# Expert loop of a mixture-of-experts stage: one bias table, other POOL slots, transposes of the next rows at other places

## The reference

```python
gu = xb @ w_gu[e] + b_gu[e]                       # (128,1024) @ (1024,2048)
g = jnp.minimum(gu[:, ::2], SWIGLU_LIMIT)
u = jnp.clip(gu[:, 1::2], -SWIGLU_LIMIT, SWIGLU_LIMIT)
h = (u + 1.0) * (g * jax.nn.sigmoid(SWIGLU_ALPHA * g))
return h @ w_dn[e] + b_dn[e]                      # (128,1024) @ (1024,1024)
```

## Time and profile before

| what | us |
|---|---|
| median of 3 runs | 3178.49 (3175.48 to 3181.2) |
| the profiled execution's own time | 3171.74 |
| its span, first to last instruction | 3169.9 |
| PE busy in the span | 2691.3 (85%) |
| DVE busy | 1818.4 (57%) |
| ACT busy | 1352.0 (43%) |
| POOL busy | 963.4 (30%) |
| the 32 items, about | 1694 to 3077 |

### The profile page before, as it was taken

The page is one execution under the profiler, slowest core; times in us unless marked ns, Lnnn a source line. Parts: engine busy times, 40 slices in busy tenths (PEclk is TensorE's granted clock), DMA queues, the critical chain, the costliest instruction groups (busy, mean ns, idle before and its releaser), DMA issues. The chain is left out here.

```text
span 3169.9 us, 37221 instructions
## 1 busy us (share of the span) xinstructions
PE 2691.3 (85%) x13181; PEld 1995.3 (63%) x13181; DVE 1818.4 (57%) x2326; ACT 1352.0 (43%) x1417; POOL 963.4 (30%) x435
## 2 busy tenths in 40 slices
PE   7698999799969999797836999999999999999970
PEld 4465555689945555586334777777777777776750
DVE  0433444317755555210245877777877777777766
ACT  1232322214334444100004666666666666666650
POOL 0001121000012222000023555555555555555553
PEclk9899999799989999898957999999999999999995
DMA  2103343222232112332027888889889889889854
GB/s 79 56 1 120 132 166 117 56 69 81 67 98 83 31 57 57 93 80 98 25 74 270 315 319 320 314 310 322 310 320 321 311 311 321 307 324 320 307 202 162
DMA packets 240551, 580.65 MB, mean 183 GB/s; under 512 B 25660, under 2 KB 114812, under 8 KB 235336
## 3 DMA queue, kind: packets, MB, share of 16 engines
q1 hardware_dynamic: 221984, 503.18, 46.5%
q0 software_dynamic: 17168, 76.05, 6.5%
q10 hardware_dynamic: 1296, 0.01, 0.0%
HBM read 546.88 MB, written 32.18 MB: 183 GB/s over the span
## 5 line engine op out<-in xcount | busy, mean ns | idle before, releaser
L2048 ACT ACTIVATE w_hi<-w_raw 128x2048 fp32r<-128x2048 f32 x290 | 556.5, 1919 | 241.0 <-PE banks L1994 241.0
L2089 DVE TENSOR_TENSOR w_lo<-w_raw,w_hi 128x2048 fp32r<-128x2048 f32 x226 | 570.2, 2551 | 120.0 <-ACT w_hi L2048 120.0
L1994 PE MATMUL banks<-w_hi,x_hi 128*128 128x512 f32 x1024 | 349.4, 424 | 96.4 <-POOL b_two L1953 89.7
L1958 POOL TENSOR_TENSOR w_lo<-w_raw,w_hi 128x2048 fp32r<-128x2048 f32 x64 | 302.1, 4721 | 344.9 <-ACT w_hi L2048 344.9
L1994 PE MATMUL banks<-w_hi,x_lo 128*128 128x512 f32 x1024 | 337.2, 412 | 0.0
L1994 PE MATMUL banks<-w_lo,x_hi 128*128 128x512 f32 x1024 | 334.9, 410 | 0.0
L1994 PEld LDWEIGHTS banks<-w_hi,x_hi 128*128 128x128 f32 x1024 | 206.1, 207 | 162.9 <-issue 121.7
L2089 DVE TENSOR_TENSOR w_lo<-mergedT,w_hi 128x2048 fp32r<-128x2048 f32 x98 | 233.5, 2410 | 104.5 <-ACT w_hi L2048 104.5
L2048 ACT ACTIVATE w_hi<-mergedT 128x2048 fp32r<-128x2048 f32 x98 | 187.8, 1917 | 182.5 <-PE banks L1994 117.9
L1994 PEld LDWEIGHTS banks<-w_lo,x_hi 128*128 128x128 f32 x1024 | 206.0, 201 | 46.8
L1994 PEld LDWEIGHTS banks<-w_hi,x_lo 128*128 128x128 f32 x1024 | 204.5, 200 | 45.6
(11 more groups left out here) (399 smaller groups left out, 5087.0 us busy)
## 6 DMA issues: line engine op xcount, KB each, us to landing
w_raw<-in_exp_w_gu SPq DMA_DIRECT2D x194, 1024.0 KB, 6.0
w_raw<-in_exp_w_down SPq DMA_DIRECT2D x96, 1024.0 KB, 7.2
mergedT<-in_exp_w_gu SPq DMA_DIRECT2D x66, 1024.0 KB, 8.3
mergedT<-in_exp_w_down SPq DMA_DIRECT2D x32, 1024.0 KB, 6.8
w_x<-in_w_in SPq DMA_DIRECT2D x12, 1024.0 KB
out<-h SPq DMA_DIRECT2D x20, 512.0 KB
wz<-in_w_in SPq DMA_DIRECT2D x4, 2048.0 KB
h<-in_state_ssm SPq DMA_DIRECT2D x16, 512.0 KB
```

Of the source, the lines that this page charges most:

```text
L1958: pool.tensor_tensor(w_lo[:, s % NHI], raw(s, par), w_hi[:, s % NHI].bitcast(F32), ALU.subtract).then_inc(lo_p, 1)
L1994: mm = pe.matmul(banks[:, bank + c, :], x[:, k, :], part[:, j, c * 512:(c + 1) * 512], start=start, stop=False)
L2048: act.activation(w_hi[:, s % NHI], raw(s, par), ACT.Copy).then_inc(hi_ready, 1)
L2089: dve.tensor_tensor(w_lo[:, s % NHI], raw(s, par), w_hi[:, s % NHI].bitcast(F32), ALU.subtract).then_inc(lo_v, 1)
```

## The change

- **Bias table.** `stage_route` loads all 32 experts' biases twice (64 rows x 3072), ACT makes the high parts of all 64 rows and POOL overwrites the lower 32 rows with raw minus high. In the loop, POOL builds a one-hot of 64 x 128 for the next item's expert (`choose`), and `add_bias` multiplies it with the table. The loads, conversions and subtraction of each item go, and with them PE's wait at the item's start.
- **POOL's waits.** POOL no longer waits for its gather or its scatter to land; ACT waits for the scatter before the copy into `y_out`. POOL reads the expert's number with a register load in each item. The table of row numbers is copied in two parts, one for the gather and one for the scatter. One scatter of whatever `y_out` holds is sent before the loop (its rows are written again later).
- **POOL's slots** are 4 and 9 in place of 10 and 11. POOL's order is low 4, gather, choose, low 9, scatter.
- **Transposes.** X0 and X1 go to banks 0 and 1. H0 is turned after slot 5, H1, X0 and X1 in the middle of slot 9. PE waits for X1's low part at an item's start.
- **Orders.** ACT: 4 to 7, sigmoid 0, 8, H0, 9, 10, 11, sigmoid 1, next 0, H1, X0, X1, next 1 to 3, output copy. DVE: 5, 6, clamp 0, gate 0, 7, 8, H0, 10, clamp 1, gate 1, 11, H1, X0, X1, next 0 to 3. Before, DVE had low 7 between clamp 0 and gate 0, and H0's low part between clamp 1 and gate 1.

The core of the diff:

```diff
+    c[:2 * E, K_PICK:K_PICK + E] = (r % E == np.arange(E)[None, :])[:2 * E]
...
+                for p0 in (0, E):
+                    sp.dma_start(b_raw[p0:p0 + E, 0:2 * FF], io.bgu).then_inc(b_in, 16)
+                    sp.dma_start(b_raw[p0:p0 + E, 2 * FF:3 * D], io.bdn).then_inc(b_in, 16)
                 sp.wait_ge(zeroed, 2)
...
+                pool.wait_ge(b_high, 1)
+                pool.wait_ge(zeroed, 2)
+                pool.tensor_tensor(sb.b_all[E:2 * E], b_raw[E:2 * E], sb.b_all[E:2 * E].bitcast(F32), ALU.subtract).then_inc(b_low, 1)
+                pool.wait_ge(b_low, 1)
                 pool.wait_ge(cleared, 16)
...
+                act.wait_ge(b_in, 64)
+                act.activation(sb.b_all, b_raw, ACT.Copy).then_inc(b_high, 1)
                 act.wait_ge(expd, 1)
...
-    POOL_SLOTS = (10, 11)
+    POOL_SLOTS = (4, 9)
...
+        U_H0, U_H1, U_X0, U_X1 = range(4)
+        TURN_BANK = {U_H0: 6, U_H1: 7, U_X0: 0, U_X1: 1}
...
+        def expert(eng, it):
+            return eng.value_load(sb.item_expert[0:1, bass.ds(it, 1)], min_val=0, max_val=E - 1)
...
                 def run(it, par):
-                    e, e_next = expert(it), expert(it + 1)
+                    e, e_next = expert(sp, it), expert(sp, it + 1)
                     for s in range(AHEAD, NW):
                         load(e, it, s, par)
-                        if s == 7:
-                            biases(e_next, it + 1, 1 - par)
                     for s in range(AHEAD):
...
+                    pool.tensor_copy(from_row[:, par:par + 1, :], sb.tok[:, bass.ds(it, 1), 0:1]).then_inc(from_put, 1)
+                    pool.wait_ge(from_put, it + 1)
                     if not isinstance(it, int):
-                        pool.wait_ge(turned, it * 4 - 2)
+                        pool.wait_ge(turned, turns(it - 1, U_X1))
                     pool.sem_inc(carried, 1)
                     pool.indirect_dma_start(out=x_raw, out_offset=None, in_=io.h_rows,
-                                            in_offset=bass.IndirectOffsetOnAxis(ap=index[:, par, 0:1].bitcast(U32), axis=0)).then_inc(x_in, 16)
-                    pool.wait_ge(x_in, it * 16 + 16)
-
...
+                                            in_offset=bass.IndirectOffsetOnAxis(ap=from_row[:, par, :].bitcast(U32), axis=0)).then_inc(x_in, 16)
+
+                def choose(e, par):
+                    pool.tensor_copy(pick[:, par, :], K[0:2 * E, bass.ds(e + K_PICK, 1)].broadcast_to((2 * E, P))).then_inc(picked, 1)
 
...
-                def run(it, par):
-
-                    gather(it + 1, 1 - par)
-                    for s in POOL_SLOTS:
-                        low(it, s, par)
-                    split_biases(it + 1, 1 - par)
+                def scatter(it, par):
+                    pool.tensor_copy(to_row[:, par:par + 1, :], sb.tok[:, bass.ds(it, 1), 1:2]).then_inc(to_put, 1)
+                    pool.wait_ge(to_put, it + 2)
                     pool.wait_ge(y_copied, it + 2)
                     pool.sem_inc(carried, 1)
-                    pool.indirect_dma_start(out=io.y_rows, out_offset=bass.IndirectOffsetOnAxis(ap=index[:, par, 1:2].bitcast(U32), axis=0),
+                    send(par)
+
+                def send(par):
+                    pool.indirect_dma_start(out=io.y_rows, out_offset=bass.IndirectOffsetOnAxis(ap=to_row[:, par, :].bitcast(U32), axis=0),
                                             in_=y_out, in_offset=None).then_inc(y_stored, 16)
-                    pool.wait_ge(y_stored, it * 16 + 16)
-                    pool.sem_inc(y_free, 1)
-
-                pool.sem_inc(b_split, 2)
-                pool.sem_inc(y_free, 1)
+
+                def run(it, par):
+                    e_next = expert(pool, it + 1)
+                    low(it, 4, par)
+                    gather(it + 1, 1 - par)
+                    choose(e_next, 1 - par)
+                    low(it, 9, par)
+                    scatter(it, par)
+
                 gather(0, 0)
-                pool.wait_ge(picked, 2)
-                split_biases(0, 0)
-                items(pool, run)
+                choose(0, 0)
+                pool.tensor_copy(to_row[:, 1, :], K[:, K_PAIR:K_PAIR + 1]).then_inc(to_put, 1)
+                pool.wait_ge(to_put, 1)
+                send(1)
+                n = items(pool, run)
+                pool.wait_ge(y_stored, n * 16 + 16 * (E + 1))
 
...
                 def add_bias(par, bank, row):
                     for c in range(2):
-                        mm = pe.matmul(banks[:, bank + c, :], pick[:, row + c, :], b_two[:, par, :], start=False, stop=True)
+                        mm = pe.matmul(banks[:, bank + c, :], pick[:, par, :], sb.b_all[:, (row + c) * 512:(row + c + 1) * 512], start=False, stop=True)
                     return mm
 
                 def run(it, par):
-                    pe.wait_ge(b_split, it + 3)
+                    pe.wait_ge(turned_lo, turns(it, U_X1))
                     for h in range(2):
                         pe.wait_ge(gu_read, it * 2 + h + 1)
                         for q in range(4):
@@ -2009,33 +2000,34 @@
                             for j in range(2):
                                 mm = products(4 * h + q, j, x_hi, x_lo, 2 * q + j, 2 * h, q == 0 and j == 0)
                             mm.then_inc(w_used, 1)
+                            if h == 1 and q == 1:
+                                pe.wait_ge(hid_ready, it * 2 + 1)
+                                turn(U_H0, hid, 0)
+                        if h == 0:
+                            pe.wait_ge(picked, it + 1)
                         add_bias(par, 2 * h, 2 * h).then_inc(gu_ready, 1)
-                    pe.wait_ge(hid_ready, it * 2 + 2)
-                    turn(it + 1, U_H0, hid, 0)
-                    pe.wait_ge(x_in, it * 16 + 32)
-                    turn(it + 1, U_X0, x_raw, 0)
                     pe.wait_ge(y_copied, it + 1)
                     for q in range(4):
-                        if q == 1:
-                            turn(it + 1, U_X1, x_raw, 4)
-                            pe.wait_ge(hid_ready, it * 2 + 3)
-                            turn(it + 1, U_H1, hid, 4)
+                        if q == 0:
+                            pe.wait_ge(turned_lo, turns(it + 1, U_H0))
                         if q == 2:
                             pe.wait_ge(turned_lo, turns(it + 1, U_H1))
-                        if q == 0:
-                            pe.wait_ge(turned_lo, turns(it + 1, U_H0))
                         wait_low(pe, it, 8 + q)
                         for j in range(2):
+                            if q == 1 and j == 1:
+                                pe.wait_ge(hid_ready, it * 2 + 2)
+                                turn(U_H1, hid, 4)
+                                pe.wait_ge(x_in, it * 16 + 32)
+                                turn(U_X0, x_raw, 0)
+                                turn(U_X1, x_raw, 4)
                             mm = products(8 + q, j, h_hi, h_lo, 2 * q + j, 4, q == 0 and j == 0)
                         mm.then_inc(w_used, 1)
                     add_bias(par, 4, 4).then_inc(y_ready, 1)
 
                 pe.sem_inc(w_used, NW)
-                pe.wait_ge(picked, 2)
                 pe.wait_ge(x_in, 16)
-                turn(0, U_X0, x_raw, 0)
-                turn(0, U_X1, x_raw, 4)
-                pe.wait_ge(turned_lo, 2)
+                turn(U_X0, x_raw, 0)
+                turn(U_X1, x_raw, 4)
                 items(pe, run)
...
                     for s in range(AHEAD, 8):
                         high(it, s, par)
                     sigmoid(it, 0)
-                    for s in range(8, NW - 1):
-                        high(it, s, par)
+                    high(it, 8, par)
                     turned_high(it + 1, U_H0, h_hi, 0)
+                    high(it, 9, par)
+                    high(it, 10, par)
+                    high(it, 11, par)
                     sigmoid(it, 1)
+                    high(it + 1, 0, 1 - par)
+                    turned_high(it + 1, U_H1, h_hi, 4)
                     turned_high(it + 1, U_X0, x_hi, 0)
-                    high(it, NW - 1, par)
                     turned_high(it + 1, U_X1, x_hi, 4)
-                    turned_high(it + 1, U_H1, h_hi, 4)
-                    for s in range(AHEAD):
+                    for s in range(1, AHEAD):
                         high(it + 1, s, 1 - par)
                     act.wait_ge(y_ready, it + 1)
-                    act.wait_ge(y_free, it + 1)
+                    act.wait_ge(y_stored, it * 16 + 16)
                     act.activation(y_out, banks[:, 4:6, :].rearrange("p c n -> p (c n)"), ACT.Copy).then_inc(y_copied, 1)
...
                 def clamp(it, h):
                     pair = banks[:, 2 * h:2 * h + 2, :].rearrange("p c (f t) -> p c f t", t=2)
                     two = lambda t: t.rearrange("p (c f) -> p c f", c=2)
                     dve.wait_ge(gu_ready, it * 2 + h + 1)
...
```

(49 more changed lines are left out.)

37 lines of the change are left out of this document (3 added, 34 removed).

## The result

The changed kernel takes 3101.49 us (3098.08 to 3104.05, 4 runs) against 3177.53 us for the kernel before (median of the runs beside it): a ratio of 0.9762, 95% interval 0.975 to 0.9774. It is faster by 76 us.

What follows compares the result with a forecast made beforehand. The bound was the chain POOL low 11, bias split, PE, with PE itself next. Items falling from 43.2 to 42.0 us give -37 over 31 periods, plus -2 once only: 3178.5 - 39 = 3139 us, range 3108 to 3170.

Steps and rivals of the forecast that it cites:

- rival A: The stall at slot 9 stays but the clock holds; item 39.6 us, time 3065; chance 0.15.
- The split and the start wait: At an item's start, PE's 2.9 us wait for POOL's bias split goes; lower clock there had cost 1.9 us.
- H0's 1.05 us: PE's 1.05 us wait for H0's low part goes, with H0 turned after slot 5 and needed at slot 8.
- Low 4 fits: POOL's low 4 runs from T + 5.2 to T + 9.8, before PE needs it at T + 11.76.
- Wait for hid of h = 0: Low 4 holds DVE's low 5, so PE waits 0 or 0.7 us for hid at H0, mean 0.3.
- Low 9 holds low 10: POOL's low 9 delays DVE's low 10 to T + 28.2; PE waits 2.7 us mid slot 9 (2.1 to 2.9).
- The clock behind it: PE's clock drops after the slot 9 stall, costing 1.4 us an item, bounds 0 and 1.9.
- The base: An item takes 37.3 us without both waits at full clock, plus 0.2 for a third group of transposes.
- The sum: Per item 37.3 + 0.2 + 0.3 + 2.7 + 0.1 + 1.4 = 42.0 us against 43.2; -37 us over 31 periods.
- Once only: Outside the periods: router stage +1, loop start -1.5, loop end -1.5, sum -2 us.
- C: Slower: a late scatter delays POOL's low 4, giving PE a second long stop at H0; item 44.4, time 3213; chance 0.18.
- Rival B: No stall replaces the old one, low 9 slipping in during DVE's clamps; item 37.5 us, time 3000; chance 0.08.

Runs made afterwards that it cites:

- e1: The kernel before with the bias table alone, old POOL slots, orders, landing waits and transpose places kept; 3021.7 us, ratio 0.9517.
- h1: e2 with H0 turned at its old place, behind h = 1's bias, and ACT's and DVE's orders to match; 3058.7 us, ratio 0.9619.
- e2: The changed kernel with DVE's low 10 moved behind gate 1 and low 11 behind H1's low part; 2995.8 us, ratio 0.9433.
- e3: The changed kernel with slot 9's low part on DVE, POOL keeping slot 4 alone; 3017.4 us, ratio 0.9507.
- g1: The changed kernel with POOL's low 9 written as two subtractions of 1024 columns; 3025.0 us, ratio 0.9521.
- f4: e2 with no low part on POOL, DVE making all 12; 2980.8 us, ratio 0.9373.
- e4: The changed kernel with POOL's waits for its gather and its scatter to land put back; 3333.7 us, one run.
- f1: e1 without POOL's landing waits, ACT waiting for the scatter before the output copy; 3021.1 us, ratio 0.9505.

## Why the prediction was right

The change makes the kernel faster, the old stop goes, and a new, shorter one stands in its place, at slot 9 and for the forecast reason. The size is another matter. The gain is 76 us where 39 was forecast, 3101 lies under the forecast's own 3108 to 3170, and it is as far from the forecast's 3139 as from rival A's 3065. Nearly every term was taken too large.

- **The split and the start wait** (2.9 and 1.9 us an item): right, and shown by e1, 4.86 us.
- **H0's 1.05 us**: right that it goes. The item before and the changed one differ in much else; h1 shows a wait of 1.49 us at the old place.
- **Low 4 fits**: right. It started at T + 5.6 (T = 2029.26) and ended at T + 10.2, against 5.2 and 9.8. The register load, put at 0.5 us between the two, took 0.29 and ran while the scatter was under way.
- **Wait for hid of h = 0**, 0.3 us in mean: did not come. Hid was there at T + 17.2 in this item (2046.47) and at T + 16.7 in the next, PE came to it at T + 17.3. The forecast had T + 17.9 for items with a table load, but that load ran under the clamp, at 2042.40. In e2, where the scatter is slower, the wait came, with 0.41 us.
- **Low 9 holds low 10**: right. Low 10 ended at T + 28.3, forecast 28.2; the wait was 2.37 us in mean, forecast 2.7 with 2.1 as the lower bound. Shown by e2, e3 and g1 from three sides.
- **The clock behind it**, 1.4 us in mean: too high. A fall costs 1.4, but it came in 23 of 31 items, which makes 1.0. What is left, 40.94 - 37.14 (f4's item, without any wait) - 2.37 - 1.0 = 0.4, is there with the clock up too (39.67 - 2.10 - 37.14) and was forecast only as H1's 0.1: H1's low part holds slot 10 by 0.12 us, and the last pair of matmuls before the stop (2057.02) takes 0.61 us where pairs start 0.45 apart; the remainder of it was not traced. That clock and rest together again make 1.4 is luck.
- **The base**, 37.3 + 0.2: too high. f4 is the measured floor, 37.14. The 0.2 was for three groups of transposes in place of two, which is a misreading: there are two groups before (eight and eight) and two after (H0's four, then twelve).
- **The sum**: base 0.36, H0 0.3, stop 0.33 and clock 0.4 too much, 0.3 too little for the rest, make the 1.1 us by which the item was forecast too long (42.0 against 40.94). Over 31 periods these 33 us are nearly all of 3139 against 3101. The terms were mis-sized; the chain was right.
- **Once only**, -2 us: measured -1.3 and -4.1. POOL's subtraction in the router stage took 6.67 us from 1614.80 and so ended 0.25 us ahead of DVE's first step on the logits at 1621.72, which came 17.9 us after the stage's start as before: nothing, where +1 was taken. Of the -4.1 at the end, 1.2 is the scatter that follows the last copy sooner; the rest was not traced.
- **Slips that nothing rests on**: the tables are 64 x 3072 x 4 bytes, 0.79 and not 0.77 MB, and C's own terms add up to 41.9 before the clock, not 42.1.

Rival A had the stop without the clock: that is 8 of 31 items, so the truth lies between A and the forecast. Rival B's item of 37.5 us is what a kernel without the stop takes (e2 37.72, f4 37.14), it only is not this kernel. C's second stop came in full in e4 alone; its way, a scatter that waits for a DVE low and so a later low 4 and a later hid of h = 0, shows in e2 with 0.41 us. The loads did not bind: f4 moves 367 GB/s over a millisecond. That is over the 358 GB/s of the Trainium skill's HBM Reference, Specifications (TRN2), and its item is under the 38.1 us worked out from that figure; the page's own remark, that a core alone goes above its share, agrees.

Not tried: the changed orders with each item's bias split kept, so whether the new orders alone would gain over the kernel before stays open.

## What to carry to other kernels

Give POOL elementwise work on SBUF only where DVE has PSUM work or nothing: in these runs a DVE operation with two SBUF inputs that met a POOL subtraction stood until that was over, and with it all that was queued behind. Here the kernel with no such work on POOL at all was the fastest. When a wait on the bound engine is removed, look for the engine order that puts a held instruction ahead of the result that the bound engine needs next; here two lows moved back in DVE's order were worth 106 us, more than the whole change (76). Try each part of a large change alone: the table was worth 156 us, and the parts beside it took half of that back.

## What the runs showed that was not expected

- Behind a wait of PE of 1.49 us (h1) the clock fell to its lower level in 13 of 31 items and cost 1.6 us there, more than the wait itself, while waits of 1.05 us (e1, f1) and of 0.83 and 1.34 in turns (g1) left it at 1.00. In the changed kernel, with 2.10 and 2.64 us in turns, it fell in 23 of 31.
- Giving DVE two more lows of 2.28 us an item (f4) shortened the item by 0.58 us against e2, though DVE's busy share rose from 88% to 93%.
- The removal of POOL's landing waits is worth nothing with POOL's slots 10 and 11 (3021.7 and 3021.1 us) and 232 us with slots 4 and 9 (3333.7 and 3101.5 us): the same edit, at two places.
